# A layer's attention with another order inside each step: exponential before the turned tile, products one step earlier

## The reference

```
def attend(i):                      # one tile of 128 queries
    sc = einsum(qn, k_nope) + einsum(qr, k_rope)
    sc = where(causal, sc * scale, -inf)
    p = softmax(sc)
    return einsum('bhqk,bkhd->bqhd', p, v)
```

## Time and profile before

| | us |
|---|---|
| median of 3 runs (2471.14 to 2476.09) | 2472.5 |
| profiled execution, its time | 2471.14 |
| its span | 2469.3 |
| TensorE busy | 2341.7 (95%) |
| VectorE busy | 983.4 (40%) |
| ScalarE busy | 859.0 (35%) |
| POOL busy | 339.0 (14%) |

### The profile page before, as it was taken

One profiled execution on the slowest core, in us unless ns is written; L12 is line 12 of the kernel. 1 busy time (PEld: TensorE's weight loads), 2 busy tenths in 40 slices (PEclk: granted clock), 3 DMA queues, 4 the chain that ended last, 5 costly groups with the idle time before them and its releaser, 6 DMA issues.

```text
span 2469.3 us, 25993 instructions
## 1 busy us (share of the span) xinstructions
PE 2341.7 (95%) x10629; PEld 1940.8 (79%) x10629; DVE 983.4 (40%) x1089; ACT 859.0 (35%) x1233; POOL 339.0 (14%) x372
## 2 busy tenths in 40 slices
PE   7999999999997999899999788989999999999997
PEld 6888888888786877688887677767888888888885
DVE  3334433432335554211213788465342233322333
ACT  3322223322223666411323566344332223222222
POOL 0000000200003232200012455332210000200002
PEclk9999999999999999999999899999999999999998
DMA  5333433443232111122410100445433423343221
GB/s 179 93 104 100 139 94 94 128 128 102 87 98 77 47 39 48 52 77 68 122 40 20 27 14 21 171 162 167 123 103 102 137 94 94 121 130 107 94 100 62
DMA packets 278016, 232.55 MB, mean 94 GB/s; under 512 B 22853, under 2 KB 250250, under 8 KB 277898
## 3 DMA queue, kind: packets, MB, share of 16 engines
q1 hardware_dynamic: 277898, 230.89, 30.3%
HBM read 209.36 MB, written 20.97 MB: 93 GB/s over the span
## 4 chain that ended last, share of the span: by engine, by line
PE 80%; issue 7%; POOL 5%; DVE 4%; ACT 3%; DMA 1%; SPq 0%; POOLq 0%; ACTq 0%; DVEq 0%
PE ps L85 26%; PE ps L86 26%; PE ps L87 26%; POOL r_xc L841 1%; PE ps L320 1%; POOL r_xc L835 1%; POOL r_xc L838 1%; PE ps L1459 1%; PE ps L1491 1%; ACT a_probs L1435 1%; POOL a_rot L1376 1%; POOL b_sum L1631 1%; ACT w_hi L91 0%; POOL x L287 0%; DVE a_s L1425 0%
## 5 line engine op out<-in xcount | busy, mean ns | idle before, releaser
L85 PE MATMUL ps<-u_hi,w_hi 128*128 128x512 f32 x1920 | 753.0, 392 | 15.5 <-ACT r_gate_y L761 9.5
L87 PE MATMUL ps<-u_hi,w_lo 128*128 128x512 f32 x1920 | 750.9, 391 | 0.0
L86 PE MATMUL ps<-u_lo,w_hi 128*128 128x512 f32 x1920 | 750.8, 391 | 0.0
L95 DVE TENSOR_TENSOR w_lo<-w_raw,w_hi 128x1024 fp32r<-128x1024 f32 (+2 forms) x345 | 426.4, 1239 | 687.9 <-ACT w_hi L91 687.7
L91 ACT ACTIVATE w_hi<-w_raw 128x1024 fp32r<-128x1024 f32 (+2 forms) x345 | 355.3, 1033 | 492.2 <-PE ps L87 452.8
L85 PEld LDWEIGHTS ps<-u_hi,w_hi 128*128 128x128 f32 x1920 | 363.1, 189 | 93.4 <-issue 15.6
L87 PEld LDWEIGHTS ps<-u_hi,w_lo 128*128 128x128 f32 x1920 | 362.5, 189 | 76.1
L86 PEld LDWEIGHTS ps<-u_lo,w_hi 128*128 128x128 f32 x1920 | 362.7, 189 | 74.5
L85 PE MATMUL ps<-w_hi,hs 128*128 128x512 f32 x704 | 275.3, 391 | 12.9 <-DVE hs L95 9.6
L86 PE MATMUL ps<-w_lo,hs 128*128 128x512 f32 x704 | 274.6, 390 | 0.0
L87 PE MATMUL ps<-w_hi,hs 128*128 128x512 f32 x704 | 274.5, 390 | 0.0
(11 more groups left out here) (213 smaller groups left out, 2449.8 us busy)
## 6 DMA issues: line engine op xcount, KB each, us to landing
w_raw<-in_ffn_w_gate_dram SPq DMA_DIRECT2D x88, 512.0 KB, 3.8
w_raw<-in_ffn_w_up_dram SPq DMA_DIRECT2D x88, 512.0 KB, 3.7
w_raw<-in_ffn_w_down_dram SPq DMA_DIRECT2D x88, 512.0 KB, 3.4
w_raw<-in_w_in_dram SPq DMA_DIRECT2D x32, 512.0 KB, 3.8
w_raw<-in_w_out_dram SPq DMA_DIRECT2D x24, 512.0 KB, 3.5
x<-in_x_dram SPq DMA_DIRECT2D x16, 512.0 KB, 6.3
h_scratch<-x SPq DMA_DIRECT2D x16, 512.0 KB, 5.0
x<-h_scratch SPq DMA_DIRECT2D x16, 512.0 KB, 5.2
```

What stands on the lines that cost most here:

```text
L85: pe.matmul(out, lh, rh, start=start, stop=False)
L86: pe.matmul(out, lh, rl, start=False, stop=False)
L87: return pe.matmul(out, ll, rh, start=False, stop=stop)
L95: return nc.vector.tensor_tensor(lo, src, as_f32(hi), ALU.subtract)
```

## The change

Inside each step the order is another on every engine. TensorE now issues scores, the unit, the product, the transposes of n-2 (before: product, scores, transposes, unit). ScalarE now issues the exponential of n, the unit, the rope of the unit before, the high part of n-2, the copy of the product (before: copy, high part, rope, exponential, unit). VectorE now issues the maximum, the unit, the rope, the low part of n-2, the add (before: add, maximum, low part, rope, unit). POOL normalises first and adds the rope of the same step's unit behind it.

Units come earlier in a head: steps 0, 1, 3, 4 instead of 1, 3, 6, 7 in odd heads, and 1, 3 instead of 1, 7 in even ones. The products come at steps 6 and 2 instead of 7 and 3, the split of a pair with them, and the split of the unit's weights at step 5 of one head instead of step 2 of the next. The slots of blocks 4 to 7 of a transposed tile are taken in ascending order instead of descending.

```
-        at = {1: 0, 3: 1, 6: 2, 7: 3} if h % 2 else {1: 0, 7: 1}
+        at = {0: 0, 1: 1, 3: 2, 4: 3} if h % 2 else {1: 0, 3: 1}
...
-                at = s - j if b else j
-                last = pe.transpose(c.ps[:, 4 + b, at * P:(at + 1) * P], self.prob(n)[:, j * P:(j + 1) * P], c.ident[:, :])
+                last = pe.transpose(c.ps[:, 4 + b, (j % 4) * P:(j % 4 + 1) * P], self.prob(n)[:, j * P:(j + 1) * P], c.ident[:, :])
...
-        count = min(4, s + 1 - 4 * b)
-        first = 4 - count if b else 0 if s < 4 else 4
+        count, first = min(4, s + 1 - 4 * b), 0 if s < 4 or b else 4
...
-            unit, first = (j, j) if m == 0 else (4 + j, 0) if j < 4 else (7 - j, j - 4)
+            unit, first = (j, j) if m == 0 else (4 + j, 0) if j < 4 else (j - 4, j - 4)
...
     def act_step(self, act, n):
         h, s = n // HEAD_TILES, n % HEAD_TILES
-        if s == 7:
-            self.take(act, h, 0)
-        if s == 3 and h > 0:
-            self.take(act, h - 1, 1)
-        if n >= 2:
-            self.turned_hi(act, n - 2)
-        if s == 3 and h > 0 and h % 2 == 0:
-            self.pair_hi(act, h // 2 - 1, slice(0, SEQ), 2 * h)
-        if n == HEADS * HEAD_TILES - 1:
-            self.pair_hi(act, 3, half_of(0), 2 * HEADS - 1)
         if n < HEADS * HEAD_TILES:
-            if n > 0 and self.beside(n - 1):
-                self.rope_act(act, self.beside(n - 1))
             self.exponent(act, n)
             if self.beside(n):
                 self.unit_act(act, self.beside(n))
+            if n > 0 and self.beside(n - 1):
+                self.rope_act(act, self.beside(n - 1))
+        if n >= 2:
+            self.turned_hi(act, n - 2)
+        if s == 6:
+            self.take(act, h, 0)
+        if s == 2 and h > 0:
+            self.take(act, h - 1, 1)
+            if h % 2 == 0:
+                self.pair_hi(act, h // 2 - 1, slice(0, SEQ), 2 * h)
+        if n == HEADS * HEAD_TILES - 2:
+            self.pair_hi(act, 3, half_of(0), 2 * HEADS - 1)
...
         if n < HEADS * HEAD_TILES:
             self.maximum(dve, n)
+            if self.beside(n):
+                self.unit_dve(dve, self.beside(n))
+            if n > 0 and self.beside(n - 1):
+                self.rope_dve(dve, self.beside(n - 1))
         if n >= 2:
             self.turned_lo(dve, n - 2)
...
     def pool_step(self, pool, n):
-        if n > 0 and self.beside(n - 1):
-            pool.wait_ge(self.S["norm_done"], n)
-            self.rope_pool(pool, self.beside(n - 1))
         self.normalise(pool, n)
+        if self.beside(n):
+            pool.wait_ge(self.S["norm_done"], n + 1)
+            self.rope_pool(pool, self.beside(n))
...
-        if s == 7:
+        self.scores(pe, n)
+        if self.beside(n):
+            self.unit_of(pe, self.beside(n))
+        if s == 6:
             self.product(pe, h, 0)
-        if s == 3 and h > 0:
+        if s == 2 and h > 0:
             self.product(pe, h - 1, 1)
-        self.scores(pe, n)
         if n >= 2:
             self.turn(pe, n - 2)
-        if self.beside(n):
-            self.unit_of(pe, self.beside(n))
...
-                    if n % HEAD_TILES == 2 and 0 < n // HEAD_TILES < HEADS:
-                        w.hi(act, heads[n // HEAD_TILES + 3])
+                    if n % HEAD_TILES == 5 and n // HEAD_TILES < HEADS - 1:
+                        w.hi(act, heads[n // HEAD_TILES + 4])
```

More of the change, by code:

```diff
@@ L1549, in dve_step @@
     def dve_step(self, dve, n):
         h, s = n // HEAD_TILES, n % HEAD_TILES
-        if s == 7:
-            self.add(dve, h, 0)
-        if s == 3 and h > 0:
-            self.add(dve, h - 1, 1)
         if n < HEADS * HEAD_TILES:
             self.maximum(dve, n)
+            if self.beside(n):
+                self.unit_dve(dve, self.beside(n))
+            if n > 0 and self.beside(n - 1):
+                self.rope_dve(dve, self.beside(n - 1))
         if n >= 2:
             self.turned_lo(dve, n - 2)
-        if n < HEADS * HEAD_TILES:
-            if n > 0 and self.beside(n - 1):
-                self.rope_dve(dve, self.beside(n - 1))
-            if s == 3 and h > 0 and h % 2 == 0:
+        if s == 6:
+            self.add(dve, h, 0)
@@ L1563, in dve_step @@
+        if s == 2 and h > 0:
+            self.add(dve, h - 1, 1)
+            if h % 2 == 0:
                 self.pair_lo(dve, h // 2 - 1, slice(0, SEQ), h // 2)
-            if n == HEADS * HEAD_TILES - 1:
-                self.pair_lo(dve, 3, half_of(0), 4)
-            if self.beside(n):
-                self.unit_dve(dve, self.beside(n))
+        if n == HEADS * HEAD_TILES - 2:
+            self.pair_lo(dve, 3, half_of(0), 4)
     def pool_step(self, pool, n):
-        if n > 0 and self.beside(n - 1):
-            pool.wait_ge(self.S["norm_done"], n)
-            self.rope_pool(pool, self.beside(n - 1))
@@ L2232, in _ @@
                     att.dve_step(dve, n)
-                    if n % HEAD_TILES == 2 and 0 < n // HEAD_TILES < HEADS:
-                        w.lo(dve, heads[n // HEAD_TILES + 3])
+                    if n % HEAD_TILES == 5 and n // HEAD_TILES < HEADS - 1:
+                        w.lo(dve, heads[n // HEAD_TILES + 4])
                 att.add(dve, HEADS - 1, 1)
```

## The result

The change makes the kernel slower: 2542.85 us in the median of four runs (2539.04 to 2543.4) against 2472.8 (2471.14 to 2476.09), a ratio of 1.0279 with a 95% interval of 1.0261 to 1.0297. The profiled execution took 2538.51 us (span 2536.7), 67.4 more than before. The forecast was 2545, range 2510 to 2585.

The account below looks back on a forecast made before the run. TensorE was taken as busy for 95% of the span, with VectorE also nearly full in the attention. A serial ScalarE-VectorE chain and a lower clock were added: 2471.1 + 59 + 15 = 2545 us, range 2510 to 2585.

Parts of the forecast that it names:

- lo, max, exp, hi: VectorE's low part and maximum, ScalarE's exponential and high part run serially each attention step: 22.8 us per bare head.
- three signs in the waits: In attention, ScalarE waits for the maximum and VectorE for the high part in most steps; TensorE waits before products.
- The sum of +59: Attention: eight heads total 257 us on the serial chain, so the last exponential ends at 1619.6 instead of 1560.84.
- The second product's +3.3: Step 2: product of a head's second half, transpose, high part, copy and add take 5.1 us against a bare 1.8.
- the pair split's +2.35: End of step 2 in even heads: the split waits for the add, then runs on ScalarE and VectorE, nothing beside: +2.35 us.
- The clock, +15: Attention: TensorE, 65% busy instead of 88%, gets a lower granted clock; a third of 44 us taken, 15 us.
- upper bound: All TensorE work on the chain at half clock: seven products 22 us, odd-head query units 12, even-head 10; 44 in all.
- Merge and the rest: Behind the attention the merge runs as now, and everything outside the attention lasts as before.
- Gaps filled: Rival: the unit ahead of the transposes covers TensorE's 20.7 us of waits and half-clock stretches go: 2456 us, chance 4%.
- no effect: Rival: the change leaves the time as it is, 2471 us; chance 2%.
- only products and pair splits cost (2501): Rival: ScalarE and VectorE still overlap in plain steps; only product and pair split cost, 30 us: 2501, chance 10%.
- Half clock throughout (2600): Rival: TensorE at half clock throughout needs 87 us a pair of heads, more than the chain's 67: 2600 us, chance 10%.

Follow-up runs that it names:

- scores_twice: Changed kernel with every scores matmul of the attention issued twice, 46 us more TensorE work at full clock: 2539.04 us, ratio 1.0277.
- exp_twice_after: Changed kernel with every exponential run twice in a row on ScalarE, a semaphore between the two: 2583.37 us, ratio 1.0453.
- old_products: Changed kernel with products, copies, adds and pair splits back at steps 7 and 3, with descending slots: 2524.94 us, ratio 1.0219.
- hi_first: Changed kernel with ScalarE doing the high part of tile n-2 ahead of the exponential of n again: 2569.85 us, ratio 1.0402.
- max_ahead: Changed kernel with VectorE reducing the maximum of tile n+1 ahead of the low part of tile n-2: 2579.5 us, ratio 1.0436.
- exp_twice_before: Kernel before the change with every exponential run twice in a row on ScalarE, a semaphore between: 2506.26 us, ratio 1.0142.

## Why the prediction came out right, step by step

**What bounds before, and the line in the new order.** Right as far as the changed kernel goes. The predicted line lo, max, exp, hi is there row by row, with hand-overs of about 0.03 us (the exponential of 1523.52 follows a maximum that began at 1522.41 and took 1.08). All three signs in the waits came: ScalarE for the maximum 62 times of 64, VectorE for the high part, TensorE 20.0 us before the products. scores_twice confirms that TensorE is off the line in the plain steps, exp_twice_after that ScalarE is on it.

**The sum of +59.** Right within the resolution that the clock leaves. Head 1 is the one at full clock (0.99) with all terms of an odd head: 34.76 us against 34.4 worked out. Head 0 was forecast at 27.7 from the first maximum and took 26.4 to the next head's first exponential, 1.3 less; head 7, 28.0 with the last hi and lo, took 26.46 + 1.7 = 28.2. Two terms can be read alone, from one exponential to the next at step 2: 5.27 us in head 1, where 5.1 were worked out for the step with the second product, and 7.77 in head 4, 2.5 more for the pair split, where 2.35 were. Even heads were forecast at 32.7 and took 34.9 to 35.1, odd ones behind head 1 36.1 and 36.5. The second product's +3.3, the pair split's +2.35 and the first product's +0.5 make 7 x 3.3 + 3 x 2.35 + 8 x 0.5 = 34 us for steps 2 and 6; old_products, which puts the products back where they have other steps around them, gives back 18 of it. It was expected that not all would go, since the copies, adds and splits stay on the line at the later steps.

**The clock, +15.** The mechanism is there, its size was too large: 7 to 8 us. What TensorE did before each fall to the lower level (0.50, that is 1.2 GHz) stands in its timeline. Seven times, at steps 0 and 4 of heads 2, 4 and 6 and at step 0 of head 7, it had stood idle for 3.2 to 3.4 us; within 2 us of the end of the wait the clock was down, for 3 to 7 us. In odd heads units at steps 0 and 4 break up these waits, and none is longer than 1.96 us. Yet heads 3 and 5 each have one fall, behind two waits of 1.7 and 1.6 us with 1.4 us of matmuls between, while head 1 has the same two waits and stayed up; one more came in head 0 behind waits of 1.48 and 1.96. Single waits of 2 us ahead of the products had none behind them.

A fall costs time where TensorE is on the line, above all at the query unit of step 1. In heads 3 and 5 this step takes 6.05 and 6.29 us, in head 1, with the same instructions at full clock, 4.72. In even heads the trace shows it directly, here at head 4, in TensorE's timeline, the window and VectorE's timeline:

```profile
1495.41 1.28 PE L1458 MATMUL ps<-ident,a_probs 128*128 128x128 f32 x7 [3.42 <-DVE a_pt L95]
...
1497.22 0.78 PE L85 MATMUL ps<-cq,w_hi 128*128 128x512 f32 x1
...
1500.10 0.40 PE L87 MATMUL ps<-cq,w_lo 128*128 128x512 f32 x1
1500.34 1.03 PE L1458 MATMUL ps<-ident,a_probs 128*128 128x128 f32 x8
...
1504.03 3.32 PE L1488 MATMUL ps<-a_pt,a_v 128*128 128x512 f32 x16 [2.06 <-DVE a_pt L95]
```

```profile
1495.46:1498.87 3.41, 3.41 (x15) 3.03 (x16) 1.82 (x5) 1.93 (x6) 1.37 (x3) 0.56 0.00 0
1498.87:1502.29 3.42, 3.10 (x18) 2.47 (x17) 1.69 (x3) 1.70 (x4) 1.24 (x3) 0.93 0.02 5
```

```profile
1500.54 0.68 DVE L1357 TENSOR_TENSOR a_rot<-ps,trig 32x512 f32<-32x512 f32 x1 [2.24 <-PE ps L87]
```

The unit takes from 1497.22 to 1500.34, 3.1 us instead of the 2.1 at full clock, in a stretch with a clock of 0.56 in which TensorE never stood idle, and VectorE waits 2.24 us for its end. In scores_twice the same step of head 2 ran at 1.00, and VectorE waited half as long, although TensorE had 0.36 us more of scores ahead of the unit:

```profile
1429.70 0.68 DVE L1357 TENSOR_TENSOR a_rot<-ps,trig 32x512 f32<-32x512 f32 x1 [1.03 <-PE ps L87]
```

So 1.2 to 1.6 us of an even head are clock, and the remaining 0.7 to 1.0 is a wait that the prediction did not have in even heads at all. Three even heads at 1.2 to 1.6, the two odd ones at 1.3 and 1.6 and 0.4 at step 0 of head 7 make 7 to 8. The falls at step 4 are the longest (0.53 from 1516.2 to 1523.4) and cost nothing that shows: steps 4 and 5 of head 4 take 3.73 and 4.20 us, and 3.74 and 4.20 in scores_twice at a clock of 1.00. The largest term of the upper bound, seven products at half clock, did not come: all seven took 3.30 to 3.36, as at full clock. In that bound of 44 the 10 us for three units of the even heads do not follow from the 2.1 us of a unit either, which give 6.3; and the third taken of it was a choice, not a measurement.

Against the forecast without clock, 257 - 1.7 = 255.3 from the first maximum to the last exponential, the 265.1 measured are 9.8 more: 7 to 8 of clock, 2 to 3 of the even heads' wait, 1 of the odd heads, less the 1.3 of head 0. The closeness of the total is partly luck. The forecast started from the profiled execution, and its 2545 stand against that of the changed kernel, 2538.51: the line was worked out at 59 and came at 60, with two small errors against each other, and the clock at 15 and came at 7 to 8. The median of 2542.85 happens to lie nearer.

The Trainium skill (TensorE: Matmul & The Clock Gate, HAM oscillation) describes a kernel whose bursts of matmuls are parted by waits of some 3 to 5 us for transfers, and in which every burst starts at half clock. The trace of after agrees for waits of that length, seven of 3.2 to 3.4 us with seven falls; of its shorter waits, up to 2.06 us, most had none behind them.

**Merge and the rest.** Right: 67.8 us within the attention, 67.4 in the span.

**The signs.** A pair over 67 us came. "PEclk below 0.9 in the attention's slices" did not in those words: the windows of pairs show 0.90 to 0.93, and of heads 1 to 6 only the even ones alone are below.

**The rivals.** Gaps filled and no effect fall with the time. That only products and pair splits cost (2501) falls with the step shown above: its 4.26 us are serial apart from the copy, and only the 0.60 of the add belong to a product; and old_products, with the products back in their place, keeps 53 of the 71 us. Half clock throughout (2600) falls with the windows: 0.85 to 0.99 for heads 1 to 6.

**What was wrong in the reasons.** "The decisive part is the order on ScalarE" holds for the kernel before, where that move alone costs 82 us, but it is not what has to be undone: hi_first takes it back and loses another 27, part of it by the clock. TensorE's new order was costed at little ("it only waits elsewhere"). With the transposes behind unit and product, any order of ScalarE or VectorE that waits for TensorE early turns into a line through three engines, as hi_first and max_ahead show. Not tried was TensorE's old order in the changed kernel with all else left, so how much of the 35 us it carries by itself stays open.

## What to carry to other kernels

When several engines take a pipelined loop in fixed order, follow one step from hand-over to hand-over around the engines and sum it: work that stands side by side costs the larger, work that stands in a line costs the sum, and busy shares tell neither. An order that is balanced across engines changes as a whole; a move on one engine, or its removal from a new order, can cost more than the full change, so test a part from both sides. A term with a clock in it is read from one period at full clock and the excess over it of others with the same instructions.

## What was not expected of the hardware

46 us more work for TensorE cost nothing and raised its clock from 0.90 to 0.93 up to 0.95 to 0.98 in the same pairs (scores_twice). The kernel as a whole became neither faster nor slower: heads 3 and 5 came 1.1 and 1.5 us shorter, head 6 came 1.6 longer, and the line through VectorE and ScalarE stayed.

In the changed kernel the lower level shows in stretches of work, as in the earlier trace rows: 0.56 over 3.41 us in which TensorE was wholly busy, behind a wait of 3.42 us in which the clock still stood at 1.00. That does not mean that it falls on work. In old_products TensorE stands idle from 1438.52 to 1443.85; the window of the first 3.2 us shows 0.99, that of the last 2.0 shows 0.50. So the wait ahead of a slow stretch is to be read with it, and the stretch's own busy time says little.

A semaphore between two instructions of ScalarE itself was nearly free: in exp_twice_before the second exponential starts at 1503.05, 0.04 us behind the end of the first at 1502.00 + 1.01.
